# Order of ScalarE's work in the expert loop: down weights' high halves, scaling and sigmoid moved

## What is computed

```python
def expert_block(args):
    xblk, e = args                                  # one block of rows, all of one expert
    gu = xblk @ w_gu[e] + b_gu[e]                   # w_gu[e]: 1024 x 2048, float32
    gate = jnp.minimum(gu[:, ::2], SWIGLU_LIMIT)
    up = jnp.clip(gu[:, 1::2], -SWIGLU_LIMIT, SWIGLU_LIMIT)
    act = (up + 1.0) * gate * jax.nn.sigmoid(SWIGLU_ALPHA * gate)
    return act @ w_down[e] + b_down[e]              # w_down[e]: 1024 x 1024, float32
```

## Time and profile before

| | us |
|---|---|
| median of 3 executions | 3023.1 |
| profiled execution | 3036.56 |
| its span, first to last instruction | 3034.7 |
| PE busy in the span | 2651.0 (87%) |
| DVE busy | 1792.5 (59%) |
| ACT busy | 1539.7 (51%) |
| POOL busy | 716.7 (24%) |
| low halves, gate-and-up (L1591, 256 times) | 601.0 |
| high halves, gate-and-up (L1080, 256 times) | 516.3 |
| low halves, down (L1596, 128 times) | 284.6 |
| high halves, down (L1086, 128 times) | 235.8 |

### The profile page before, as it was taken

One profiled execution on the slowest core, in us unless ns is written; L12 is line 12 of the kernel. 1 busy time (PEld: TensorE's weight loads), 2 busy tenths in 40 slices (PEclk: granted clock), 3 DMA queues, 4 the chain that ended last, 5 costly groups with the idle time before them and its releaser, 6 DMA issues. The chain is left out here.

```text
span 3034.7 us, 131520 instructions
## 1 busy us (share of the span) xinstructions
PE 2651.0 (87%) x55749; PEld 2284.3 (75%) x55749; DVE 1792.5 (59%) x2083; ACT 1539.7 (51%) x1822; POOL 716.7 (24%) x572
## 2 busy tenths in 40 slices
PE   8999988989898895799979999798999988789973
PEld 2444547888788444799879898798999988789863
DVE  2353984454543466667786627867173567773784
ACT  3423534333343334566775526766263566773773
POOL 1211004454442011122122212212122212222222
PEclk9999998999999996999999999999999999999996
DMA  9400001100001226667697617969173568784795
GB/s 368 161 28 30 1 8 32 25 17 24 17 24 38 105 83 250 241 233 275 241 377 285 231 28 282 379 241 349 28 256 128 194 224 322 287 312 133 266 371 183
DMA packets 124466, 536.84 MB, mean 177 GB/s; under 512 B 12524, under 2 KB 13536, under 8 KB 91600
## 3 DMA queue, kind: packets, MB, share of 16 engines
q1 hardware_dynamic: 107104, 481.80, 41.9%
q0 software_dynamic: 14464, 47.79, 7.1%
q10 hardware_dynamic: 2832, 6.37, 0.6%
HBM read 496.99 MB, written 38.92 MB: 177 GB/s over the span
## 5 line engine op out<-in xcount | busy, mean ns | idle before, releaser
L2068 PE MATMUL ps<-qkv,weights 128*128 128x64 f16 x10496 | 976.9, 195 | 166.4 <-DVE qkv L1629 68.4
L2068 PEld LDWEIGHTS ps<-qkv,weights 128*128 128x128 f16 x10496 | 939.7, 99 | 185.4 <-issue 100.8
L2069 PE MATMUL ps<-qkv,weights 128*128 128x64 f16 x10496 | 976.1, 195 | 9.3 <-issue 7.2
L2070 PE MATMUL ps<-qkv,weights 128*128 128x64 f16 x10496 | 976.0, 195 | 6.6 <-issue 5.3
L2069 PEld LDWEIGHTS ps<-qkv,weights 128*128 128x128 f16 x10496 | 940.5, 99 | 11.8 <-issue 11.8
L2070 PEld LDWEIGHTS ps<-qkv,weights 128*128 128x128 f16 x10496 | 940.6, 99 | 9.7 <-issue 9.7
L1591 DVE SCALAR_TENSOR_TENSOR weights<-hT,weights 128x2048 f16<-128x2048 f32 x256 | 601.0, 2402 | 207.2 <-ACT weights L1080 203.8
L1080 ACT ACTIVATE weights<-hT 128x2048 f16<-128x2048 f32 x256 | 516.3, 2082 | 72.3 <-DMA hT<-in_w_gu_dram 42.3
L2085 PE MATMUL ps<-qkv,weights 128*128 128x64 f16 x5248 | 476.7, 193 | 12.6 <-DVE weights L1596 11.3
L2086 PE MATMUL ps<-qkv,weights 128*128 128x64 f16 x5248 | 476.5, 193 | 4.2 <-issue 4.2
L2087 PE MATMUL ps<-qkv,weights 128*128 128x64 f16 x5248 | 476.6, 193 | 0.0
(11 more groups left out here) (357 smaller groups left out, 4023.2 us busy)
## 6 DMA issues: line engine op xcount, KB each, us to landing
hT<-in_w_gu_dram SPq DMA_DIRECT2D x256, 1024.0 KB, 15.8
qkv<-in_w_down_dram SPq DMA_DIRECT2D x128, 1024.0 KB
weights<-in_w_ada_dram SPq DMA_DIRECT2D x12, 2048.0 KB, 17.1
qkv<-in_w_in_dram SPq DMA_DIRECT2D x4, 2048.0 KB, 7.6
hT<-decay_rows SPq DMA_DIRECT2D x20, 256.0 KB, 3.4
hT<-beta_rows SPq DMA_DIRECT2D x20, 256.0 KB, 4.0
qkv<-in_x_dram ACTq DMA_DIRECT2D x8, 512.0 KB, 6.5
weights<-in_w_in_dram SPq DMA_DIRECT2D x2, 2048.0 KB, 14.7
```

Of the source, the lines that this page charges most:

```text
L2068: pe.matmul(dst, ghi[k][:, b, c], xT[:, 0, k, :], start=first, stop=False, skip_group_check=True)
L2069: pe.matmul(dst, ghi[k][:, b, c], xT[:, 1, k, :], start=False, stop=False, skip_group_check=True)
L2070: last = pe.matmul(dst, glo[k][:, b, c], xT[:, 0, k, :], start=False, stop=end, skip_group_check=True)
```

## The change

In ACT's loop alone: `next_down` is now called for block t+1 in turn t, behind `scale_y(t-1)` and ahead of `high_act(t+1)`, where it was called for block t at the top of turn t; `scale_y(t-1)` stands behind the gate-and-up chunks of t+2 instead of ahead of the LATE ones; chunk 3 (`MIDDLE`) is split off from LATE and stands ahead of `sigmoid(t+1)`, chunks 4 to 7 (`LAST`) behind it; flags and ranks of t+1 and t+2 are read at the top of the turn and passed on. The calls ahead of the loop and behind it follow suit. No other engine's program changes: DVE still takes the low halves of down at the top of its turn.

```diff
--- before.py
+++ after.py
@@ -495,6 +495,7 @@
         E_AT, NEW_AT, N_AT = 0, NB, 2 * NB
         MINB = SEQ * TOPK // B
         EARLY, LATE = range(3), range(3, GK)
+        MIDDLE, LAST = range(3, 4), range(4, GK)
 
         @block.sync
         def _(sp):
@@ -1086,16 +1087,14 @@
                 act.activation(dhi[j], dstage[j].rearrange("p (j n) -> p j n", j=2), ACT.Copy,
                                scale=WSCALE).then_inc(s_dhi, 1)
 
-            def next_gate_up(t, new, part):
+            def next_gate_up(t, new, r, part):
                 with act.If(new > 0):
-                    r = rank_before(t)
                     for k in part:
                         high_gate_up(t, r, k)
                 act.sem_inc(s_idle, 1)
 
-            def next_down(t):
-                with act.If(flag(t) > 0):
-                    r = rank_before(t)
+            def next_down(t, new, r):
+                with act.If(new > 0):
                     for j in range(DK):
                         high_down(t, r, j)
                 act.sem_inc(s_idle, 1)
@@ -1170,38 +1169,40 @@
             for i in range(2):
                 act.wait_ge(s_yin[i], 16 * (5 - 2 * i))
             act.wait_ge(s_gtp, 2)
-            new = flag(1)
-            next_gate_up(1, new, EARLY)
+            new, r = flag(1), rank_before(1)
+            next_gate_up(1, new, r, EARLY)
             copy_xT(1)
             name_rows(2)
             sigmoid(0)
-            next_gate_up(1, new, LATE)
+            next_gate_up(1, new, r, LATE)
             high_act(0)
             for j in range(DK):
                 high_down(0, 0, j)
-            new = flag(2)
-            next_gate_up(2, new, EARLY)
+            new2, r2 = flag(2), rank_before(2)
+            next_gate_up(2, new2, r2, EARLY)
             copy_xT(2)
             name_rows(3)
             sigmoid(1)
-            next_gate_up(2, new, LATE)
+            next_gate_up(2, new2, r2, LATE)
+            next_down(1, new, r)
             high_act(1)
             copy_yT(0)
             with act.Fori(1, MAXB) as t:
                 with act.If(t <= nprev):
-                    next_down(t)
+                    new, r = flag(t + 1), rank_before(t + 1)
+                    new2, r2 = flag(t + 2), rank_before(t + 2)
                     act.wait_ge(s_xg, t * 16 + 48)
                     act.sem_inc(s_idle, 1)
                     name_rows(t + 3)
-                    new = flag(t + 2)
-                    next_gate_up(t + 2, new, EARLY)
+                    next_gate_up(t + 2, new2, r2, EARLY)
                     copy_xT(t + 2)
+                    next_gate_up(t + 2, new2, r2, MIDDLE)
                     sigmoid(t + 1)
+                    next_gate_up(t + 2, new2, r2, LAST)
                     scale_y(t - 1)
-                    next_gate_up(t + 2, new, LATE)
+                    next_down(t + 1, new, r)
                     high_act(t + 1)
                     copy_yT(t)
-            next_down(nlast)
             scale_y(nprev)
             copy_yT(nlast)
             scale_y(nlast)
```

## The result

The changed kernel takes 3031.8 us (median of 16 executions, 3027.2 to 3040.0) against 3025.4 for the kernel before (16 executions on the same chip): ratio 1.0021, 95% interval 1.0012 to 1.0031, 6.4 us slower. A second measurement of the same two programs gave 1.0026 [1.0016, 1.0035]. The forecast was 3030 us, 7.3 us slower than before. The sign, the size and the chain at block 38 came out as forecast; the split of the sum did not. The total was right by luck: two errors of some 14 us each cancelled, which only the experiments showed.

What follows compares the result with a forecast made beforehand. TensorE, busy 87% of the span, was taken as the bound, losing time at changes of expert. Terms +1.2 - 7.6 + 6.3 + 1.1 + 6.0 + 0.3 = +7.3 us on the 3023.1 median gave 3030 us, range 3008 to 3043.

Steps and rivals of the forecast that it cites:

- Y: scale_y on ACT, moved behind the last gate-and-up chunks; 1.1 us of ACT work, forecast to cost nothing.
- M: The one MIDDLE chunk on ACT, moved ahead of the sigmoid; 1.0 us won where VectorE comes late to the activation.
- D: Four high halves of the down weights on ACT; as rival, the change does nothing, 3023 us, sharing 0.28 with B.
- Part 2: ACT's order: Y behind the last gate-and-up chunks; H moves nowhere, cost nothing.
- Part 4: D ahead of H and C: -1.9 us per change after two-block experts, with M's gain; later starts in one-block runs.
- H: high_act on ACT; forecast unmoved by Part 2, and at block 38 delayed behind D to 2057.9.
- S: sigmoid on ACT; queues behind M, running from 1647.85 and not 1646.12 at an ordinary change.
- Part 1: M ahead of S on ACT: +0.3 us at each of four ordinary changes, 1.0 us gained where VectorE is late.
- Part 3: Flags read at the top of ACT's turn: nothing, covered by idle time; without that cover 1.1 us a turn.
- C: copy_yT on ACT; as rival, H, scatter, Y, D loop with 10 us scatter landings: 3044 us, chance 0.10.
- A: Faster: D fills ACT's free time if scatter lands 4 to 5 us after issue; 3002 us, chance 0.20 with smaller gains.
- B: No change: runs' scatters land after 6 us and gaps miss the half clock; 3023 us, chance 0.28 with rival D.

Runs made afterwards that it cites:

- D at the end of the turn: Changed kernel with the down high halves moved behind copy_yT(t), at the end of the turn: 3017.6 us, ratio 0.9935 to the kernel before.
- change, Y early: Changed kernel with scale_y(t-1) back ahead of the late gate-and-up chunks: 3044.5 us, ratio 1.0025 to the kernel before.
- Y alone: Kernel before with only scale_y(t-1) moved behind the late gate-and-up chunks: 3014.7 us, ratio 0.9928.
- the change without M: Changed kernel with chunk 3 back behind the sigmoid: 3037.2 us, ratio 1.0001 to the kernel before.
- D alone: Kernel before with only the four down high halves of block t+1 moved ahead of high_act(t+1): 3068.1 us, ratio 1.0103.
- the three kernels with the scatter first: Changed kernel with GpSimd's scatter ahead of low_act: 3009.3 us; also with chunk 3 behind the sigmoid: 3013.8; that with the down high halves split around high_act and copy_yT: 3005.4.

## Why the forecast held, and what in it was wrong

**The path of the sum.** The forecast put Y and the flags at 0, M at about -6 and D at about +13. The runs: M, Y and the flags together give -20 (D at the end of the turn), 14 more than forecast, and D on top costs +28, 15 more than forecast; in all +8 by the second measurement, 6.4 by the first. The errors cancelled, and that was luck. How the 20 us divide depends on the order in which the parts are added, since M and Y take away the same wait: Y first, -22 and then +2 for M and the flags; M first, -11 and then -8.5 for Y and the flags. So the step that failed is "Part 2: Y behind the last gate-and-up chunks ... Cost nothing": alone it gives 22 us. In the finished change it does cost nothing (change, Y early), but not for the reason given: M has taken that gain already. The mis-sized term is Part 4, D: +13 for +28 (+31 alone, and +22 on top of Y if the flags are worth nothing). A right total is no proof of the terms.

**Part 2, Y.** The working looked at where H begins (nearly right: at block 23 H comes 0.4 us later in Y alone) and where VectorE waits (the 1.97 us), but gave all of that wait to M. S and Y ahead of chunk 3 in the earlier trace rows make it: with Y gone 1.23 remain, and in the changed kernel 1.03, in which VectorE waits for nothing else ("issue" in the block 21 rows above): its own register reads, 1.0 in the forecast. And the forecast priced the subtraction's overlap only where D puts it on a down low half. The earlier trace rows had the other one in plain sight: five low halves in 12.06 us, which I used as the price of an overlap without asking what would take it away. Gate-and-up after a late activation took 17.8 us before, 16.8 with M, 16.1 with Y, 15.9 without M in the change.

**Part 1, M.** Right in kind by itself: first late low half after 1.03 us of idle time, +0.2 us at each of blocks 5, 8 and 11 (excess 0.6 before, 1.3 after; forecast +0.9), though some -10 us in all and not -6. Wrong in company, as shown above: the forecast left out that an earlier H moves GpSimd's subtraction against the low halves.

**Part 3, the flags.** No run holds them alone. They are not quite nothing: 0.22 us of "issue" on ACT ahead of chunk 3 is there in Y alone and gone in the change without M (1.23 against 1.03 us of idle time on VectorE), and the 0.61 us ahead of D in D alone is gone in the change.

**Part 4, after a two-block expert.** As forecast in mechanism, and near in size: D behind a Y that waits for y_scratch, 9.87 us for the four low halves (forecast 8.90 + 0.96), gain at 23 1.6 us and at 50 3.4 (forecast 1.9 each).

**Part 4, in a run.** Step for step at block 38, on the scale of before: H 2057.5 (forecast 2057.9), C 2058.0 (2058.4), scatter issued 2061.1 (2060.2) and Y 8.2 us behind it (7.5), gate-and-up of 40 at 2068.7 (2066.3), D of 39 from 2070.4 (2068.9), gate-and-up of 41 at 2090.1 (2088.6). The gap ahead of `down` was 6.1 us and not 8, and the granted clock fell to its lower level as in the earlier trace rows. (With the 1.5 for the half clock, which the forecast added apart, 2067.8 stands for gate-and-up of 40.) The subtraction takes 2.73 us there, because VectorE holds it off. The larger error is in what I let disappear: the wait for `copy_yT` came to 54 us, and the wait for VectorE's reads gave back only 18.5 of it. I had let it vanish in four runs of six, and there are nine such gaps, not six. At equal pace the change lost 6.3 us at 60 to 63 (forecast +2.1) but 1.5 at 38 to 41 (+2.1), 0.8 at 14 to 18 (+1.1), 0.7 at 66 to 71 (+3.3), 2.7 at 76 to 81 (+1.1), and gained 2.3 at 30 to 35; these sums hold M and Y too.

**The rivals.** A was given 0.20 and asked for 21 us; its mechanism is real and a mere change of order gives it. C's loop (scatter, Y, D) turned, but its 10 us landings did not come: behind the first block of a run Y stopped waiting 6.3 to 9.2 us after the scatter's issue, over both profiles of the change (forecast 7.5). B fell with the 0.50 of the granted clock and those landings. D fell with the single parts: M and D alone are both large, of opposite sign.

**The lock.** The Trainium skill (SBUF — State Buffer, "Who interferes with whom") says that issue order decides which of VectorE and GpSimd is blocked. The traces agree: the same subtraction costs VectorE 0.98 us when it comes 8.77 us after the low halves' start, and nothing when it comes at 9.39. Over all fourteen profiles the border is sharp: in 213 groups of five late low halves the subtraction starts at most 8.79 us after them, and they take 12.05 to 12.09 us; in the other 221 it starts at 8.81 us or later, and they take 11.10 (11.26 once). The fifth low half starts at 8.8. The prediction took the lock as one price per overlap; which side pays it is a large part of what moved this kernel.

## What to carry to other kernels

When an instruction is moved off the front of a queue, price what its old place delayed, not only what its new place delays; the move that looks free may be the one that pays. Two edits that remove the same wait do not add, and the second may shift a third engine onto a lock; test such edits alone and together. Before an order is written out by hand, follow each wait through the other engines' orders: here the cure for a late D was one swap on GpSimd.

## What was unexpected on the chip

The same program ran one profiled execution with a plain block of 18.8 us and another with 19.2 (613 against 600 matmuls in 19 us), so two single profiles can differ by more than this change. The difference is a hole of 0.3 us in PE's work (0.2 in D alone), and it goes with GpSimd's scatter. In thirteen of the fourteen profiles it stands 0.9 to 1.1 us behind the start of the scatter's issue in plain blocks: 2.8 us into the block where the scatter stands behind the subtraction, and 17.0 us into it in the three kernels with the scatter first, where the issue starts at 16.0. Why it is missing in the first profile of the change, and what makes it, no run here shows.

The subtraction of 128x512 takes 1.15 us alone and up to 3.3 us when it comes just behind the start of the fifth low half (4.4 once in D alone), and the scatter's issue 1.43 alone and up to 3.3 beside low halves. A shift of 0.6 us in the start of one GpSimd instruction moved the gate-and-up beside it by 0.9 us.
